# Delta layer: the gate tile and the first key tile multiplied in one pass over the normed stream

## The reference

```
h = (rms_norm(x, norm_mix[layer]) * (1.0 + sc1) + sh1).astype(x.dtype)
proj = h @ w_in
qkv, z, a, b = jnp.split(proj, [...], axis=-1)
qkv = jax.nn.silu(causal_depthwise_conv(qkv, conv_w))
q, k, v = jnp.split(qkv, [GDN_HK, 2 * GDN_HK], axis=-1)
beta = jax.nn.sigmoid(b)
g = -jnp.exp(a_log) * jax.nn.softplus(a + dt_bias)
```

## Time and profile before

| what | us |
|---|---|
| median of 3 runs | 3011.91 |
| lowest, highest | 3009.0, 3013.37 |
| the profiled execution | 3014.49 |
| its span in the profile | 3012.7 |
| PE busy | 2897.0 (96%) |
| DVE busy | 1436.4 (48%) |
| ACT busy | 1120.9 (37%) |

### The profile page before, as it was taken

One profiled execution on the slowest core, in us unless ns is written; L12 is line 12 of the kernel. 1 busy time (PEld: TensorE's weight loads), 2 busy tenths in 40 slices (PEclk: granted clock), 3 DMA queues, 4 the chain that ended last, 5 costly groups with the idle time before them and its releaser, 6 DMA issues. The chain is left out here.

```text
span 3012.7 us, 39596 instructions
## 1 busy us (share of the span) xinstructions
PE 2897.0 (96%) x16452; PEld 2486.5 (83%) x16452; DVE 1436.4 (48%) x1613; ACT 1120.9 (37%) x1551; POOL 119.8 (4%) x116
## 2 busy tenths in 40 slices
PE   8989999999999899999999988999999999899999
PEld 8889999998987588888777787788887887778887
DVE  5664333233513634444477745544455865643322
ACT  5444332132232324332255534343224446544321
POOL 0000000001400000000000010000001310000000
PEclk9999999999999999999999999999999999999999
DMA  4212332322222135556432220355563431033332
GB/s 130 68 40 74 89 92 77 96 94 91 70 84 70 29 94 147 165 154 179 123 101 79 75 43 29 112 158 156 163 184 102 112 98 32 21 91 97 93 87 85
DMA packets 409379, 292.70 MB, mean 97 GB/s; under 512 B 24851, under 2 KB 388180, under 8 KB 409250
## 3 DMA queue, kind: packets, MB, share of 16 engines
q1 hardware_dynamic: 403210, 286.68, 32.6%
q0 software_dynamic: 1600, 3.55, 0.7%
q10 hardware_dynamic: 4440, 0.64, 0.2%
HBM read 286.16 MB, written 4.13 MB: 96 GB/s over the span
## 5 line engine op out<-in xcount | busy, mean ns | idle before, releaser
L201 DVE TENSOR_TENSOR w_lo<-w_raw,w_hi 128x2048 fp32r<-128x2048 f32 (+3 forms) x237 | 497.8, 2101 | 525.0 <-ACT w_hi L195 524.5
L195 ACT ACTIVATE w_hi<-w_raw 128x2048 fp32r<-128x2048 f32 (+3 forms) x237 | 416.3, 1757 | 258.2 <-PE ps L282 150.4
L280 PE MATMUL ps<-ffn_h_hi,w_hi 128*128 128x264 f32 (+1 forms) x1008 | 323.5, 321 | 2.4 <-DVE w_lo L201 2.4
L282 PE MATMUL ps<-ffn_h_hi,w_lo 128*128 128x264 f32 (+1 forms) x1008 | 322.7, 320 | 0.0
L281 PE MATMUL ps<-ffn_h_lo,w_hi 128*128 128x264 f32 (+1 forms) x1008 | 321.4, 319 | 0.0
L280 PE MATMUL ps<-up_act_hi,w_hi 128*128 128x512 f32 (+1 forms) x880 | 308.2, 350 | 0.0
L282 PE MATMUL ps<-up_act_hi,w_lo 128*128 128x512 f32 (+1 forms) x880 | 307.3, 349 | 0.0
L281 PE MATMUL ps<-up_act_lo,w_hi 128*128 128x512 f32 (+1 forms) x880 | 305.7, 347 | 0.0
L280 PE MATMUL ps<-up_h_hi,w_hi 128*128 128x512 f32 x672 | 265.3, 395 | 6.4 <-DVE w_lo L201 6.4
L282 PE MATMUL ps<-up_h_hi,w_lo 128*128 128x512 f32 x672 | 265.3, 395 | 0.0
L281 PE MATMUL ps<-up_h_lo,w_hi 128*128 128x512 f32 x672 | 262.8, 391 | 0.0
(11 more groups left out here) (580 smaller groups left out, 5633.5 us busy)
## 6 DMA issues: line engine op xcount, KB each, us to landing
mod_raw<-in_w_ada_dram SPq DMA_DIRECT2D x128, 384.0 KB, 3.9
w_raw<-in_ffn_w_gu_dram SPq DMA_DIRECT2D x88, 512.0 KB, 5.3
w_raw<-in_w_ffn_in_dram SPq DMA_DIRECT2D x88, 512.0 KB, 5.3
w_raw<-in_ret_w_in_dram SPq DMA_DIRECT2D x24, 1024.0 KB, 5.1
w_raw<-in_ffn_w_down_dram SPq DMA_DIRECT2D x32, 704.0 KB, 5.0
w_raw<-in_w_ffn_out_dram SPq DMA_DIRECT2D x32, 704.0 KB, 4.7
w_raw<-in_dsw_w_in_dram SPq DMA_DIRECT2D x18, 1024.0 KB, 5.0
w_raw<-in_gdn_w_in_dram SPq DMA_DIRECT2D x16, 1024.0 KB, 5.6
```

Source lines behind the costliest of these rows:

```text
L195: self.nc.scalar.activation(self.w_hi[:, s, 0:w.size], self.raw[:, s, 0:w.size], ACT.Copy).then_inc(self.hi_ready, 1)
L201: self.nc.vector.tensor_tensor(self.w_lo[:, s, 0:w.size], self.raw[:, s, 0:w.size], self.w_hi[:, s, 0:w.size].bitcast(F32), ALU.subtract). ...
L280: nc.tensor.matmul(out, w_hi, h_hi, start=first, stop=False)
L282: return nc.tensor.matmul(out, w_lo, h_hi, start=False, stop=last)
```

## The change

The gate tile (t = 0) and the first key tile (t = 1) are given to `first_products` together, as three results: the gate rows in bank 0 and the two halves of the key tile in banks 2 and 3. For each chunk of the stream PE now does nine matmuls instead of three (chunk 0: twelve of 256 columns and three of 512), 78 in all, where before 26 stood beside the norm and 48 of tile 1 behind it. PE waits once, ahead of all, for the low part of tile 1 and for all results of the layer before to be out of PSUM. `tile_used` is counted up for tile 0 by the last gate matmul, now the third from the end, and for tile 1 by the last one. The loop over the other tiles begins with t = 2. ACT's, DVE's, GpSimd's and SP's instructions and their order are as before.

```diff
-        for t, (w, i, j) in enumerate(self.tiles):
+        def halves(t):
+            w, i, j = self.tiles[t]
+            return K.weights(w, j, K.w_hi), K.weights(w, j, K.w_lo)
+
+        pe.wait_ge(K.lo_ready, K.tile_no(*self.tiles[1]) + 1)
+        pe.wait_ge(K.psum_free, self.freed)
+        (ab_hi, ab_lo), (k_hi, k_lo) = halves(0), halves(1)
+        ends = self.norm.first_products(
+            pe, [(K.ps[0:72, 0, :], SEQ, 0, lambda c: ab_hi[:, c, :], lambda c: ab_lo[:, c, :])]
+            + [(K.ps[:, 2 + m, :], SEQ, 0, lambda c, m=m: k_hi[:, c, m * P:(m + 1) * P],
+                lambda c, m=m: k_lo[:, c, m * P:(m + 1) * P]) for m in range(2)])
+        ends[0].then_inc(K.tile_used, 1)
+        ends[2].then_inc(K.tile_used, 1)
+        for t, (w, i, j) in list(enumerate(self.tiles))[2:]:
             pe.wait_ge(K.lo_ready, K.tile_no(w, i, j) + 1)
             pe.wait_ge(K.psum_free, self.freed + t - 1)
-            hi, lo = K.weights(w, j, K.w_hi), K.weights(w, j, K.w_lo)
-            if t == 0:
-                self.norm.first_products(pe, [(K.ps[0:72, 0, :], SEQ, 0, lambda c: hi[:, c, :], lambda c: lo[:, c, :])])[-1]\
-                    .then_inc(K.tile_used, 1)
-                continue
+            hi, lo = halves(t)
             for m in range(2):
```

## The result

The changed kernel is slower by a little: 3017.61 us (median of 20 runs, 3013.78 to 3028.23) against 3012.84 (20 runs of the kernel before, 3008.09 to 3023.43). The ratio is 1.0018, with a 95% interval of 1.0011 to 1.0024: 5.4 us, between 3.3 and 7.2.

The account below looks back on a forecast made before the run. It took DVE to bound PE in the norm's second half, and PE alone to set the pace in tiles 1 and 2. Tile 3's +3.7 on the profiled 3014.5 gave 3018.2, or 3015.6 on the median; range 3010.8 to 3019.8 us.

Parts of the forecast that it names:

- the forecast's +3.7: At tile 3's start: 3.7 us later than before, at 1542.6 instead of 1538.92, carried to the end; chance 0.62.
- the rival of the late clock: Beside the norm and in tile 3: low clock 3.4 us longer, tile 3 itself slowed; +6.9, 3018.8 us; chance 0.15.
- The norm's gaps: Beside the norm: tile 1's products fill PE's gaps, DVE no longer bounds, PE 3.0 us ahead with both tiles at 1523.6.
- S: Start of the gate tile's last product: 1515.33 before, forecast 1522.9, bounds 1520.8 and 1524.5.
- What loses its cover: Ahead of tile 2: its split still waits for tile 0, so PE idles 4.0 us and tile 2 starts at S + 4.85.
- What is late next: Ahead of gather(1): gates, keep(1), conv(1), squares end at S + 18.3; PE waits up to 2.5 us; tile 3 at S + 19.7.
- rival of a kept gain: At tile 2: were its ACT and DVE work not behind tile 0's last product, 3.0 us stay won, 3008.9; chance 0.04.
- The clock behind the wait: In tile 2: 1.2 GHz after the idle costs 1.6 us, hidden in the wait for the squares, leaving 0.9; tile 3 unmoved.
- From tile 3 on: From tile 3 to the end: DVE has caught up, PE waits for nothing in those tiles and carries the 3.7 us.
- the step before: From the gate tile's last product to tile 3: forecast tile 3's start at S + 19.7.
- the moment of the rise: Beside the norm: clock goes to 2.4 GHz at about 1509.5, a draw per run; delay +1.6 to +5.3 by its bounds.
- the sum: Whole kernel: tile 3's +3.7 is the entire effect, 3018.2 on the profiled execution, 3015.6 on the median.

Follow-up runs that it names:

- e3: Changed kernel with tile 2's halves in own room, split right behind the norm, and most gates work behind silu(1) and silu(2); ratio to before 0.9996.
- e1: Changed kernel with only tile 2's halves given own room and split right behind the norm, without waiting for the gate tile; ratio to before 1.0033.
- e4: Changed kernel with eleven idle products on PE in the wait ahead of tile 2; ratio to before 1.0021.
- e7: Changed kernel with gates work moved behind silu(1) and silu(2), plus eleven idle products on PE ahead of tile 2; ratio to before 1.0006.
- e8_before_copy: Kernel before run against itself, without any edit; ratio 0.9994.
- e0_after: Changed kernel run once more, without any edit; ratio to before 1.0019.
- e2_gates_behind: Changed kernel with only the gates work, all but the copy of a and b, moved behind silu(1) and silu(2); ratio to before 1.0026.
- e6_half_gates: Changed kernel with only half the key tile beside the norm, the other half's 24 products behind it, and gates work moved later; ratio to before 0.9991.

## Why the prediction was right

It said 3015.6 us with a range of 3010.8 to 3019.8, and no difference over 0.2%. Measured were 3017.61 and a ratio of 1.0018; the interval, up to 1.0024, does not shut out a loss just over 0.2%. Of the 2.0 us that it missed by, 0.9 is that the kernel before has a median of 3012.84 over 20 runs and not 3011.91. The mechanism was right, and the traces show it; that the number came out as near as it did was in part luck, since the traces give less than the forecast's +3.7 (+2.84 to +3.27) and the ratios more (+4.5 to +5.7). A measurement also tells smaller differences apart than the 0.2% that the prediction assumed: with 20 runs of each the interval is 0.0007 to either side, so 5.4 us are clear of no change. By time alone the rival of the late clock, +6.9, is inside the interval too; the traces rule it out, as the clock never fell behind the wait for the squares in the three profiles of the change, and tile 3 came earlier than forecast. Point by point:

- **The norm's gaps.** Right, but mis-sized: S was 1522.34 instead of 1522.9, mainly because the clock rose at 1508.0 and not at 1509.5. The last chunk follows the one before it by 1522.34 - 1520.25 = 2.09 us, where nine products of 0.229 make 2.06, and PE shows no wait for DVE.
- **What loses its cover.** Right: ACT's high part at S + 0.49 (0.55 was said), tile 2 at S + 4.78 (4.85), PE idle 3.93 us (4.0), put down to DVE's low part.
- **What is late next.** Right: no idle time ahead of `keep(1)`, which came at S + 9.11 (9.27), the squares done at S + 18.06 (18.3), tile 3 at S + 19.55 (19.7). (The rows it used add up to S + 11.50 for `conv(1)`, not 11.55, which changes nothing; it came at S + 11.31.) e3 shows the cause: with both chains out of the way, the gain is kept. The prediction's rival of a kept gain named the work for tile 2 alone; e1 shows that without that work alone the gain would still be lost.
- **The clock behind the wait.** Right: it fell, for 3.40 us, and was taken in by the wait for the squares (0.9 us were to be left, 0.55 were). e4 shows that it cost nothing here, e7 what it costs without that wait. The Trainium skill's page "TensorE: Matmul & The Clock Gate" ("Loop structure matters more than you think") warns that matmuls behind a long wait, there one for a DMA, run at the lower clock; the row of 0.50 agrees, but in the change no time followed from it.
- **From tile 3 on.** The delay at tile 3 was 2.94 us in place of 3.7: 0.56 of the difference is S, 0.15 the step before, 0.03 the layer's start. PE's waits further on in the layer are as before; the two longest (what waits and for whom, us in total, times, longest) in the kernel before:

```profile
PE ps L2644 <- ACT gdn_o L2865: 6.7, 1, 6.7
PE ps L2604 <- DMA gdn_x_t<-gdn_blocks: 6.1, 1, 6.1
```

and in the changed one, so that nothing there takes the delay in:

```profile
PE ps L2653 <- ACT gdn_o L2874: 6.7, 1, 6.7
PE ps L2613 <- DMA gdn_x_t<-gdn_blocks: 5.9, 1, 5.9
```

The Trainium skill's page "TensorE: Matmul & The Clock Gate" (part 1, "What's actually happening") was weighed in the prediction for the moment of the rise, which it does not tie to the kernel's start. These runs agree with it: over all profiles the rise lay between some 2.5 us (e1_early) and 6.1 us (e8_before_copy) behind the layer's first product, and S between 17.11 and 18.06 us in the eight with all nine products of a chunk in the pass.

What stays open is the rest of the measured time. The three ratios of the change give +5.4, +5.7 and +4.5 us, its three traces +2.94, +3.27 and +2.84 at tile 3. About 2 us are thus not seen at this place. They are within the 2.7 us by which two equal kernels can differ, but all three ratios lean the same way. The step of the prediction that this concerns is the sum: it held that all of the change is to be seen at tile 3.

The traces don't settle it. The two traced executions of the kernel before took 3014.49 and 3017.21 us, 1.7 and 3.6 us over their medians, the three of the change 0.2 to 0.9 us under theirs, and the first of each differ by 2.88 us, no more than tile 3 shows. From the layer's first product to ACT's last instruction the three profiles of the change take 1.8 to 2.6 us longer than the first profile of the kernel before and 3.1 to 3.9 us longer than the second, and show no second place of loss. What stands ahead of this layer varies by as much: its first product began between 1502.35 and 1509.00 us over the profiles, in the kernel before alone at 1504.95 and 1509.00.

## What to carry to other kernels

Before work is moved into the gaps of a stage, list what ran under it where it stood: here a 4.78 us split of weights and a chain of gates, convolution and squares that ends at S + 18, both released by the last product of the tile ahead. Filling the gaps won 3.4 us and uncovered both. Two such chains hide each other, so removing one shows little; remove both, or move only as much work as leaves a cover (here half a tile, 5.5 us, covers the split of 4.78, while the chain of the squares still cost 1.12 us until the gates were moved).

## What the runs showed of the hardware

The clock differed between runs of one and the same place. In three profiles (e0_after, e2_gates_behind, e6_half_gates) it was at 2.4 GHz when the layer's first product began and fell to 1.2 GHz 0.4 to 1.0 us later, to rise again 3.4 us after that; in the others it was at 1.2 GHz from the first product on. Behind the same 3.93 us of idle PE, tile 2 ran 3.4 us at 1.2 GHz in two profiles of the change, some 5.3 in the third, 5.57 in e2. Behind the 2.16 us ahead of `gather(1)` in e4 it did not fall; behind 4.05 us in e1 it was down when the wait ended. Small idle matmuls that fill such a wait kept it at 2.4 GHz, as this stretch of e7, tile 2 behind them, shows:

```profile
1528.18:1539.06 10.88, 10.88 (x48) 8.94 (x49) 7.93 (x9) 7.99 (x9) 0.00 (x0) 1.00 0.57 161
```

PE's pace also differed at a granted clock of 1.00, and with PE busy all the time. One stretch of the kernel before ahead of this layer, first in its profile and then in that of its copy (e8_before_copy):

```profile
1140.00:1185.00 45.00, 45.00 (x199) 36.91 (x198) 21.91 (x20) 17.73 (x16) 0.00 (x0) 1.00 0.58 163
1140.00:1185.00 45.00, 45.00 (x194) 36.48 (x193) 19.60 (x19) 16.90 (x16) 0.00 (x0) 1.00 0.55 157
```

The same kernel starts 194 matmuls there instead of 199. In e2's profile PE goes on so for the last 270 us of its products: they start 0.233 us apart, where the change's profile has 0.229, which by these numbers is some 5 us. So one execution can be longer than another by as much as this change costs, far from it and with the same granted clock; the cause is not shown.
